# Program head of a four-layer trunk: vector loads moved to ScalarE's queue, vectors transposed between x's tiles, pool weight halves and y halves in turn

## The chip, the cores and the metric

The kernel runs on one core of one Trainium2 chip. The metric is the device time of one execution in microseconds, as the median of several runs. The engines are named as in the profile: PE is TensorE (PEld its weight loads), DVE is VectorE, ACT is ScalarE, POOL is GpSimd, SP is SyncE; SPq and ACTq are the instructions on SP and ACT that issue DMAs.

## The reference

A trunk of four layers on 16 meta tokens and 512 tokens of width 1024. Each layer is a mixer and a SwiGLU feed-forward, both with residual. The mixers are a pool mixer (layers 0 and 3), differential attention (layer 1) and a conformer convolution (layer 2). The program head ends in the first pool mixer:

```python
meta = jnp.broadcast_to(meta_tokens[None].astype(x.dtype), (B_, N_META, D_MODEL))
h = jnp.concatenate([meta, x], axis=1)
for i in range(DEPTH):
    mixer, j = i % N_MIXERS, i // N_MIXERS
    y = rmsnorm(h, norm_mix_g[i])
    if mixer == 0:
        y = pool_mixer(y, pool_w[j], pool_b[j], pool_scale[j])
    ...
    h = h + y
    h = h + swiglu_ffn(rmsnorm(h, norm_ffn_g[i]), ffn_w_gate[i], ffn_w_up[i], ffn_w_down[i])
return rmsnorm(h[:, N_META:], final_norm_g)

def pool_mixer(h, w, b, scale):
    # four groups of 256 channels: (trailing mean over 2, 4, 8, 16 tokens) - h, times a 256x256 matrix
    ...
    return (mixed + b) * scale
```

## The kernel before

Activations are kept transposed: `h` is [128 channels, 8 blocks x 528 tokens] in SBUF. Every product is made of three float32r products: each operand is split into a high part (`y_hi`, `w_hi`, made by ACT) and a rest (`y_lo`, `w_lo`, made by DVE), and PE multiplies high with high, high with low and low with high. Weights arrive in a ring `w_raw` of four slots; SP issues each load (`load`, L654) when the rest of the tile four before it has been made (`lo_ready`).

The program head does this. POOL clears `vec_rows` (L774) and `tok_x` (L775), builds the identity (L781) and then the band matrices of the trailing means (`bands_raw`, to L808). SP issues the rows of x in six loads (L634 to L638, token tiles 0 to 4, the last of 32 rows), then waits for `vec_zeroed` and issues twelve small loads of the norms' gains, biases and convolution taps into `vec_rows`, 50 rows of 1024 values (L644 to L649), then the four pool weights (through L654, 256 KB each), then four lambda vectors (L734) and the bias table (L736). PE runs six filler products (`unread`, L1709) and transposes x's five tiles (L1718), DVE copies each from PSUM to `h` (L3003). PE then runs six more fillers, transposes `vec_rows` into bank 7 (L1724), runs 15 fillers and waits for `vec_ready`, which DVE gives when it has copied the bank to `m.vec` (L3009). ACT meanwhile takes the sum of squares of each x tile (L2192, into `tok_x`) and splits the pool weights of groups 0 and 1 (L1795).

With `vec_ready` the pool layer begins. ACT makes `y_hi` of the eight channel blocks (L1800, a product with the norm's gain), with the splits of weights 2 and 3 behind blocks 1 and 3, and then rounds the band matrices (L1849). DVE makes the rests in the same order (L2342 for weights, L2348 for y), then the bands' rest (L2460), then the row factors, one reciprocal root for each token (`row_factors_of`, L2408 to L2411, from `token_sums`), and gives `tok_ready`. PE multiplies token tiles 0 to 2 group by group and then tiles 3 and 4 (L1034, `rows_times_weights`; the first product waits for `lo_ready` of group 0 and `y_ready` of blocks 0 and 1). When `tok_ready` is there, ACT scales each tile's result into `z_hi` (L1867), DVE makes `z_lo` (L2477). PE, after six fillers behind `z_ready` of two tiles (L1120), multiplies the z tiles with the bands (`windows`, L1073 to L1082; its first one waits for `z_ready` of four tiles), and between the blocks it begins layer 0's feed-forward (L972). DVE adds the windows to `h` (L2449). A DMA of the relative bias table goes out from ACT in that stretch (L1882, L2202), and from there on PE computes the feed-forward.

## Time and profile before

| | |
|---|---|
| median of 3 runs | 1990.15 us (1990.10 to 1990.54) |
| the profiled execution's own time | 1987.6 us |
| its span, first to last instruction | 1985.9 us |
| mean granted TensorE clock | 0.998 |
| PE busy | 1966.1 us, 99% of the span |
| DVE, ACT, POOL busy | 1573.7, 930.4, 207.7 us |

Times in the rows are microseconds from the span's start. A timeline row gives start, duration, engine, line, operation, out<-in, the count that was merged, and in brackets the idle time before it with what ended it. A row of the chain of waits gives start, duration and what the end of the program goes back to in that stretch. An idle engine costs time only where that chain passes over it.

### The profile page before, as it was taken

The page shows a single profiled execution, that of the slowest core. Times are in us where ns is not written, and L with a number is a line of the kernel's source. Part 1 is how long each engine was busy: PE and PEld are TensorE (multiplying, and loading weights), DVE is VectorE, ACT ScalarE, POOL GpSimd, SP SyncE. Part 2 cuts the span into 40 slices and gives each one's busy share as a digit, 9 for nine tenths or more (in the row PEclk, how much of TensorE's full clock was granted, in tenths as well). Part 3 has the DMA queues.
Part 4 walks back from the last instruction along what each step waited for, and adds up shares of the span by engine and source line. Part 5 has one row for each costly group of instructions (what it writes and reads, how often), then busy time and mean ns, then how long its engine had stood idle before and what let it go on. Part 6 is the DMA issues. An engine that isn't in the chain of part 4 may idle for free.

```text
span 1985.9 us, 39847 instructions
## 1 busy us (share of the span) xinstructions
PE 1966.1 (99%) x15706; PEld 1910.9 (96%) x15706; DVE 1573.7 (79%) x2188; ACT 930.4 (47%) x1475; POOL 207.7 (10%) x325
## 2 busy tenths in 40 slices
PE   9999999999999999999999989999999999999998
PEld 8999999999999999999999989999999998989997
DVE  6797788768788788877979987697778768977794
ACT  7443333346675534433447775343334454433342
POOL 5000000231111200000051212000000140000000
PEclk9999999999999999999999999999999999999999
DMA  5433243342111324233345762223343323423232
GB/s 171 140 86 106 84 127 85 92 124 65 53 57 56 91 86 128 79 90 105 91 115 126 163 131 64 86 86 106 84 127 85 113 70 106 116 76 106 86 105 96
DMA packets 305390, 196.82 MB, mean 99 GB/s; under 512 B 7450, under 2 KB 297243, under 8 KB 305012
## 3 DMA queue, kind: packets, MB, share of 16 engines
q1 hardware_dynamic: 298972, 175.08, 30.8%
q0 software_dynamic: 5104, 15.71, 3.8%
q10 hardware_dynamic: 1192, 4.34, 0.6%
q8 instruction: 84, 1.38, 0.3%
q14 instruction: 38, 0.31, 0.1%
HBM read 179.45 MB, written 6.44 MB: 94 GB/s over the span
## 4 chain that ended last, share of the span: by engine, by line
PE 87%; DVE 6%; ACT 3%; issue 3%; DVEq 1%; DMA 1%; SPq 0%; ACTq 0%
PE ps L972 43%; PE ps L1269 35%; PE ps L1380 2%; PE ps L1225 1%; DVE cv_odd L3098 1%; PE ps L1452 1%; DVE cv L3098 1%; PE ps L1082 1%; PE ps L1493 1%; PE ps L1034 1%; PE ps L1099 0%; PE ps L1481 0%; PE ps L1505 0%; DMA x_rows<-in_x 0%; DVE w_lo L2586 0%
## 5 line engine op out<-in xcount | busy, mean ns | idle before, releaser
L1269 PE MATMUL ps<-t_lo,y_hi 128*128 128x264 f32 (+1 forms) x1008 | 285.7, 283 | 0.0
L1269 PE MATMUL ps<-t_lo,w_hi 128*128 128x264 f32 (+1 forms) x1008 | 285.7, 283 | 0.0
L1269 PE MATMUL ps<-t_hi,w_lo 128*128 128x264 f32 (+1 forms) x1008 | 285.4, 283 | 0.0
L1269 PE MATMUL ps<-t_hi,y_lo 128*128 128x264 f32 (+1 forms) x1008 | 285.3, 283 | 0.0
L1269 PE MATMUL ps<-t_hi,w_hi 128*128 128x264 f32 (+1 forms) x1008 | 285.1, 283 | 0.1
L1269 PE MATMUL ps<-t_hi,y_hi 128*128 128x264 f32 (+1 forms) x1008 | 284.8, 283 | 0.0
L1927 ACT ACTIVATE w_hi<-w_raw 128x1024 fp32r<-128x1024 f32 (+1 forms) x108 | 127.8, 1201 | 329.6 <-PE ps L972 193.3
L972 PE MATMUL ps<-hid_hi,w_hi 128*128 128x264 f32 (+1 forms) x1184 | 265.3, 296 | 1.2 <-DVE hid_lo L2642 1.2
L972 PE MATMUL ps<-hid_lo,w_hi 128*128 128x264 f32 (+1 forms) x1184 | 264.6, 296 | 0.0
L972 PE MATMUL ps<-hid_hi,w_lo 128*128 128x264 f32 (+1 forms) x1184 | 264.2, 296 | 0.0
L972 PE MATMUL ps<-y_hi,w_hi 128*128 128x264 f32 (+1 forms) x1088 | 240.5, 297 | 0.6 <-issue 0.3
L972 PE MATMUL ps<-y_hi,w_lo 128*128 128x264 f32 (+1 forms) x1088 | 233.5, 291 | 0.0
L972 PE MATMUL ps<-y_lo,w_hi 128*128 128x264 f32 (+1 forms) x1088 | 233.5, 291 | 0.0
L1927 ACT ACTIVATE y_hi<-w_raw 128x1024 fp32r<-128x1024 f32 (+1 forms) x108 | 125.8, 1196 | 167.1 <-DVE w_raw L2596 133.9
L972 PEld LDWEIGHTS ps<-hid_hi,w_hi 128*128 128x128 f32 x1184 | 187.2, 188 | 7.3 <-DVE hid_lo L2642 1.6
L972 PEld LDWEIGHTS ps<-hid_lo,w_hi 128*128 128x128 f32 x1184 | 187.7, 188 | 5.5
L972 PEld LDWEIGHTS ps<-hid_hi,w_lo 128*128 128x128 f32 x1184 | 187.4, 188 | 5.7
L1269 PEld LDWEIGHTS ps<-t_hi,w_hi 128*128 128x128 f32 x1008 | 189.8, 188 | 0.6 <-DVE h L2682 0.5
L1269 PEld LDWEIGHTS ps<-t_hi,y_hi 128*128 128x128 f32 x1008 | 189.8, 188 | 0.0
L1269 PEld LDWEIGHTS ps<-t_lo,w_hi 128*128 128x128 f32 x1008 | 189.5, 188 | 0.1
L1269 PEld LDWEIGHTS ps<-t_hi,w_lo 128*128 128x128 f32 x1008 | 189.5, 188 | 0.0
L1269 PEld LDWEIGHTS ps<-t_hi,y_lo 128*128 128x128 f32 x1008 | 189.5, 188 | 0.0
(395 smaller groups left out, 4340.5 us busy)
## 6 DMA issues: line engine op xcount, KB each, us to landing
w_raw<-in_ffn_w_gate SPq DMA_DIRECT2D x88, 512.0 KB, 5.1
w_raw<-in_ffn_w_up SPq DMA_DIRECT2D x88, 512.0 KB, 4.7
w_raw<-in_ffn_w_down SPq DMA_DIRECT2D x70, 512.0 KB, 4.4
w_raw<-in_ffn_w_down SPq DMA_DIRECT2D x24, 384.0 KB, 4.4
w_raw<-in_attn_w_qkv SPq DMA_DIRECT2D x16, 512.0 KB, 3.8
w_raw<-in_conv_w_in SPq DMA_DIRECT2D x16, 512.0 KB, 4.1
w_lo<-w_raw POOLq DMA_DIRECT2D x16, 512.0 KB, 5.4
w_raw<-in_attn_w_qkv SPq DMA_DIRECT2D x16, 256.0 KB, 2.9
```

The costliest lines, as they stand in the source:

```text
L972: mm = pe.matmul(ps[:, bank + hf, 0:half], w[:, slot, col:col + P], x(hf), start=begin and w is m.w_hi and n == 0, stop=end and w is m.w_lo)
L1034: mm = pe.matmul(out, y[:, at:at + rows], w[:, (t0 + g) % SLOTS, k * 256:(k + 1) * 256], start=k == 0 and n == 0, stop=k == 1 and n == 2)
L1082: mm = pe.matmul(out[:, c0:c1], z, m.bands[0:TILE_ROWS[i], g, at:at + c1 - c0], start=i == 2 and n == 0, stop=i in (1, 4) and n == 1)
L1225: mm = pe.matmul(ps[:, 2 * g + hf, 0:HALF], w[:, (tile0 + g) % SLOTS, k * P:(k + 1) * P], x[:, at:at + HALF], start=k == 0 and n == 0, sto ...
L1269: mm = pe.matmul(ps[:, bank, 0:hw], w[:, at:at + P], b[:, t, k, 0:hw], start=k == 0 and n == 0, stop=k == 3 and n == 2)
L1380: mm = pe.matmul(bank, x, w, start=False, stop=k == LAST_F - 1 and n == 2)
L1452: mm = pe.matmul(ps[:, (4, proj_banks(par, 1))[part] + c, col:col + k1 - k0], q[rows, 0, q0:q0 + P], k[rows, 1, k0:k1], start=n == 0, stop ...
L1493: mm = pe.matmul(ps[:, 4, i * P:QT * P], v, w, start=False, stop=i == QT - 1 and x == 2)
L1927: act.activation(hi[:, sub * SUB:(sub + n_sub) * SUB], src, ACT.Copy).then_inc(s.op_hi, 1)
L3098: dve.scalar_tensor_tensor(out=sums[n % 2], in0=u, scalar=vec_col(ROW_DW + tap, c), in1=sums[n % 2], op0=ALU.mult, op1=ALU.add).then_inc(s ...
```

## The change

SP no longer issues the twelve vector loads: ACT does, before its first square, after the same wait for `vec_zeroed`. The pool weights' loads are thereby right behind x on SP. PE transposes the vectors after x's tile 2, with a semaphore of their own (`vec_turned`), before tile 3; the fillers before that transpose are gone and those behind tile 4 become 18 in place of 15. DVE copies the vectors behind tile 2's copies. ACT takes the squares of tiles 0 to 3 first; it splits each pool weight ahead of the two y blocks of its group, waits for `vec_ready` behind the first split, and takes the squares of tile 4 behind the eight y blocks. DVE's rests follow the same order.

```diff
@@ sync
-            sp.wait_ge(s.vec_zeroed, 1)
-            for row, name in ((ROW_MIX, "norm_mix_g"), ...):
-                sp.dma_start(m.vec_rows[row:row + n, :], a[name]).then_inc(s.vec_in, 16)
...
@@ tensor
                 mm.then_inc(s.rows_turned, 1)
-            unread(6)
-            pe.wait_ge(s.vec_in, 16 * 12)
-            for d in range(NB):
-                mm = pe.transpose(ps[:, 7, d * ROWS:(d + 1) * ROWS], m.vec_rows[:, d * P:(d + 1) * P],
-                                  m.ident[0:ROWS, 0:ROWS])
-            mm.then_inc(s.rows_turned, 1)
-
-            unread(15)
+                if i == 2:
+                    pe.wait_ge(s.vec_in, 16 * 12)
+                    for d in range(NB):
+                        mm = pe.transpose(ps[:, 7, d * ROWS:(d + 1) * ROWS], m.vec_rows[:, d * P:(d + 1) * P],
+                                          m.ident[0:ROWS, 0:ROWS])
+                    mm.then_inc(s.vec_turned, 1)
+
+            unread(18)
             pe.wait_ge(s.vec_ready, 1)
@@ scalar, pool_layer
-                    act.wait_ge(s.vec_ready, 1)
                     for d in range(NB):
+                        if d % 2 == 0:
+                            split_hi(tile0 + d // 2, 0, 0, cols[tile0 + d // 2])
+                        if d == 0:
+                            act.wait_ge(s.vec_ready, 1)
                         y_hi(d, H_IN, Y_POOL0, ROW_MIX + 0, 0, TOK)
-                        if d in (1, 3):
-                            split_hi(tile0 + (3 + d) // 2, 0, 0, cols[tile0 + (3 + d) // 2])
+                    row_squares(TILES - 1).then_inc(s.token_sums, 1)
                     act.wait_ge(s.band_built, 1)
@@ scalar, head
+            act.wait_ge(s.vec_zeroed, 1)
+            for row, name in ((ROW_MIX, "norm_mix_g"), ...):
+                act.dma_start(m.vec_rows[row:row + n, :], a[name]).then_inc(s.vec_in, 16)
...
             act.wait_ge(s.tok_cleared, 1)
-            for i, n in enumerate(TILE_ROWS):
+            def row_squares(i):
+                n = TILE_ROWS[i]
                 act.wait_ge(x_in[i], 32 if i == 0 else 16)
-                e = act.activation(m.row_squares[0:n, i, :], m.x_rows[0:n, i, :], ACT.Square,
-                                   accum_out=m.tok_x[0:n, i:i + 1])
-            e.then_inc(s.token_sums, 1)
-            for t in range(2):
-                split_hi(t, 0, 0, cols[t])
+                return act.activation(m.row_squares[0:n, i, :], m.x_rows[0:n, i, :], ACT.Square,
+                                      accum_out=m.tok_x[0:n, i:i + 1])
+            for i in range(TILES - 1):
+                row_squares(i)
@@ vector, pool_layer
-                    for c in (0, 1):
-                        split_lo(tile0 + c, 0, 0, cols[tile0 + c])
                     for d in range(NB):
+                        if d % 2 == 0:
+                            split_lo(tile0 + d // 2, 0, 0, cols[tile0 + d // 2])
                         y_lo(d, Y_POOL0, ROW_MIX + 0, 0, TOK)
-                        if d in (1, 3):
-                            split_lo(tile0 + (3 + d) // 2, 0, 0, cols[tile0 + (3 + d) // 2])
@@ vector, head
+                if i == 2:
+                    dve.wait_ge(s.vec_turned, 1)
+                    dve.tensor_copy(m.vec[:, :], ps[:, 7, 0:NB * ROWS]).then_inc(s.vec_ready, 1)
             e.then_inc(s.h_ready, NB)
-            dve.wait_ge(s.rows_turned, TILES + 1)
-            dve.tensor_copy(m.vec[:, :], ps[:, 7, 0:NB * ROWS]).then_inc(s.vec_ready, 1)
-            dve.drain()
+            dve.wait_ge(s.vec_ready, 1)
```

## Rows read from the trace of the kernel before

**Rows 1.** Chain of waits in order of time, to 120 us

```profile
2.67 7.40 DMA x_rows<-in_x
...
11.82 1.53 PE ps L1709 x12
...
14.02 0.58 DVE vec L3009
14.63 1.36 ACT y_hi L1800 x2
15.99 0.52 ACT w_hi L1795
...
20.79 2.73 ACT bands L1849
...
25.94 2.12 ACT z_hi L1867 x2
...
31.35 1.29 DVE z_lo L2477
...
32.69 0.39 PE ps L1073
...
59.22 58.65 PE ps L972 x480
```

**Rows 2.** Timeline of PE

```profile
10.12 1.70 PE L1718 MATMUL ps<-ident,x_rows 127*128 127x127 f32 x16 [1.10 <-DMA x_rows<-in_x]
...
13.91 3.62 PE L1709 MATMUL ps<-ones 128*128 128x128 f32 x30
17.58 0.35 PE L1034 MATMUL ps<-w_hi,y_hi 128*128 128x256 f32 x1
...
31.74 0.89 PE L1120 MATMUL ps<-z_hi 128*128 128x264 f32 x6
```

**Rows 3.** Timeline of ACT, its DMA issues (ACTq) among it

```profile
11.16 1.04 ACT L2192 ACTIVATE row_squares<-x_rows 32x1024 f32<-32x1024 f32 x1
...
13.24 1.36 ACT L1795 ACTIVATE w_hi<-w_raw 128x512 fp32r<-128x512 f32 x2 [0.95 <-DMA w_raw<-in_pool_w]
...
23.86 0.35 ACTq L1859 DMA_DIRECT2D bands_scratch<-bands  x1
...
31.94 1.11 ACT L1867 ACTIVATE z_hi<-ps,tok_r 32x1024 fp32r<-32x1024 f32 x1 [0.62 <-PE ps L1034]
...
54.36 0.53 ACTq L1882 DMA_DIRECT2D rel_once<-rel  x1
```

**Rows 4.** Timeline of DVE

```profile
7.31 3.56 DVE L3003 COPY h<-ps 128x512 f32<-128x512 f32 x6 [7.31 <-PE ps L1718]
11.24 1.68 DVE L3003 COPY h<-ps 128x508 f32<-128x508 f32 x4 [0.38 <-PE ps L1718]
...
27.09 2.48 DVE L2477 SCALAR_TENSOR_TENSOR z_lo<-ps,tok_r,z_hi 128x1024 fp32r<-128x1024 f32 x2 [0.40 <-ACT z_hi L1867]
```

**Rows 5.** Timeline of POOL and of SP's queue: `vec_rows` cleared, first vector load, pool weights' loads

```profile
0.81 0.94 POOL L774 MEMSET vec_rows<- 50x1024 f32 x1 [0.29 <-POOLq L3212]
...
3.63 0.38 SPq L644 DMA_DIRECT2D vec_rows<-in_norm_mix_g  x1
...
7.52 1.93 SPq L654 DMA_DIRECT2D w_raw<-in_pool_w  x4
```

**Rows 6.** Stretches: start:end, length, busy (PE, PEld, DVE, ACT, POOL), PEclk, DMA share, GB/s

```profile
3.00:8.50 5.50, 5.50 (x33) 5.50 (x34) 1.19 (x2) 3.11 (x4) 5.14 (x36) 1.00 1.02 381
8.50:10.25 1.75, 0.65 (x6) 0.41 (x5) 1.75 (x5) 1.55 (x5) 1.62 (x5) 1.00 1.06 152
1162.20:1166.30 4.10, 0.10 (x2) 0.00 (x0) 2.40 (x5) 3.24 (x9) 0.00 (x0) 1.00 1.09 261
1166.30:1172.00 5.70, 5.63 (x66) 5.66 (x68) 5.67 (x10) 5.65 (x7) 0.83 (x2) 0.70 0.05 9
```

**Rows 7.** Page, DMA issues: KB each, median us from issue to landing

```profile
lam_rows<-in_attn_lambda_k SPq DMA_DIRECT2D x2, 32.0 KB, 6.3
```

More of the change, by code:

```diff
@@ L367, in __init__ @@
         self.rows_turned = sem("rows_turned")
+        self.vec_turned = sem("vec_turned")
         self.turned_read = sem("turned_read")
@@ L638, in _ @@
                 sp.dma_start(m.x_rows[0:n, i, :], a["x"][0, t:t + n, :]).then_inc(x_in[i], 16)
-            sp.wait_ge(s.vec_zeroed, 1)
-            for row, name in ((ROW_MIX, "norm_mix_g"), (ROW_FFN, "norm_ffn_g"), (ROW_POOL_B, "pool_b"),
-                              (ROW_POOL_S, "pool_scale"), (ROW_DWB, "conv_dw_b"), (ROW_LNG, "conv_ln_g"),
-                              (ROW_LNB, "conv_ln_b"), (ROW_CONV_OUT, "conv_b_out")):
-                n = a[name].shape[0]
-                sp.dma_start(m.vec_rows[row:row + n, :], a[name]).then_inc(s.vec_in, 16)
-            sp.dma_start(m.vec_rows[ROW_CONV_IN:ROW_CONV_IN + 2, :],
-                         a["conv_b_in"].rearrange("o (r n) -> (o r) n", r=2)).then_inc(s.vec_in, 16)
-            for t, n in ((0, 16), (16, TAPS - 16)):
-                sp.dma_start(m.vec_rows[ROW_DW + t:ROW_DW + t + n, :], a["conv_dw_w"][0, t:t + n, :]).then_inc(s.vec_in, 16)
-            sp.dma_start(m.vec_rows[ROW_SUBLN:ROW_SUBLN + 1, 0:P], a["attn_subln_g"]).then_inc(s.vec_in, 16)
             def load(off, i, per, src, at_col, width):
@@ L2186, in attention_step @@
                         split_hi(first["attn_out"] + NB + c, 0, 0, 512)
+            act.wait_ge(s.vec_zeroed, 1)
+            for row, name in ((ROW_MIX, "norm_mix_g"), (ROW_FFN, "norm_ffn_g"), (ROW_POOL_B, "pool_b"),
+                              (ROW_POOL_S, "pool_scale"), (ROW_DWB, "conv_dw_b"), (ROW_LNG, "conv_ln_g"),
+                              (ROW_LNB, "conv_ln_b"), (ROW_CONV_OUT, "conv_b_out")):
+                n = a[name].shape[0]
+                act.dma_start(m.vec_rows[row:row + n, :], a[name]).then_inc(s.vec_in, 16)
+            act.dma_start(m.vec_rows[ROW_CONV_IN:ROW_CONV_IN + 2, :],
+                         a["conv_b_in"].rearrange("o (r n) -> (o r) n", r=2)).then_inc(s.vec_in, 16)
+            for t, n in ((0, 16), (16, TAPS - 16)):
+                act.dma_start(m.vec_rows[ROW_DW + t:ROW_DW + t + n, :], a["conv_dw_w"][0, t:t + n, :]).then_inc(s.vec_in, 16)
+            act.dma_start(m.vec_rows[ROW_SUBLN:ROW_SUBLN + 1, 0:P], a["attn_subln_g"]).then_inc(s.vec_in, 16)
             act.wait_ge(s.tok_cleared, 1)
-            for i, n in enumerate(TILE_ROWS):
+            def row_squares(i):
+                n = TILE_ROWS[i]
                 act.wait_ge(x_in[i], 32 if i == 0 else 16)
-                e = act.activation(m.row_squares[0:n, i, :], m.x_rows[0:n, i, :], ACT.Square,
-                                   accum_out=m.tok_x[0:n, i:i + 1])
-            e.then_inc(s.token_sums, 1)
-            for t in range(2):
-                split_hi(t, 0, 0, cols[t])
+                return act.activation(m.row_squares[0:n, i, :], m.x_rows[0:n, i, :], ACT.Square,
+                                      accum_out=m.tok_x[0:n, i:i + 1])
+            for i in range(TILES - 1):
+                row_squares(i)
             pool_layer("pool0", 0, R_POOL0, Y_POOL0, H_POOL0, Y_FFN0, ROW_FFN + 0)
```

## The prediction

> **What bounds the kernel now.** The page has PE busy for 99% of the span, so only a stretch in which the end does not depend on PE's own work can give time back. I read the chain of waits of the first 120 us to find such stretches, then the timelines of PE, ACT and DVE over the same time to see how close the next engine is, and last SP's queue with the stretches of DMA traffic.
>
> The chain [rows 1] begins with the load of x's tile 3, landed at 10.07 (2.67 + 7.40). It goes through the transposes of tiles 3 and 4 [rows 2], six fillers that take 1.53 before the vectors are transposed, and DVE's copy of the vectors (0.58) to `vec_ready`. At 14.63 it enters ACT and stays: y blocks and two weight splits to 20.79, the bands for 2.73, a short row-factor chain on DVE, `z_hi` from 25.94, the fourth `z_lo` (ends 32.64), and only then PE's windows at 32.69. From there PE runs with next to no gap into the long stretch at 59.22 [rows 1]. PE's first pool product, at 17.58 [rows 2], is not in the chain at all. PE ends that stage at 31.74, and its six fillers, some 0.7 us, bring it to about 32.5, so it has only a few tenths to spare against the 32.69 of the chain.
>
> The quantity to forecast is therefore when the fourth `z_lo` is ready. It comes 32.64 - 14.63 = 18.01 after the first `y_hi`.
>
> **What the change does to ACT between the first y_hi and z_hi.** Before, weights 0 and 1 were split while ACT waited for the vectors (it began at 13.24), and the square of tile 4 was done at 11.16 [rows 3]. Now the split of weight 1 stands behind the first two y blocks and the square behind the last. A split in a row of ACT's work takes 0.52 (the one at 15.99, [rows 1]), and the square 1.04 [rows 3]. The bands, and the row factors that need the tile's sum as well, wait behind them. The fourth `z_lo` then comes 18.01 + 0.52 + 1.04 = 19.57 after the first `y_hi`. To be as early as now, 32.64, the first `y_hi` must begin at 13.07: 1.56 earlier than now. All the saving at the top of the program has to pay this first.
>
> DVE does as many rests as before; in its new order each pair follows ACT's pair and the bands' rest follows ACT's bands, so it adds nothing to this chain.
>
> **When the first y_hi can begin.** It needs three things; the last one decides.
>
> (a) All of `h`. DVE's copies of tiles 3 and 4 end 11.24 + 1.68 = 12.92 [rows 4], which is 2.85 after tile 3 of x lands at 10.07. The next instruction on ACT starts some 0.06 later, so this says 12.98 plus whatever tile 3 is late.
>
> (b) DVE's own order. Tiles 0 to 2 end at 7.31 + 3.56 = 10.87 [rows 4]. The vectors' copy of 0.58 [rows 1] now comes next, and the last copies take 1.68: 13.13, or 13.19 with the same 0.06. The copy used to run alone behind them; in the old gap of 0.38 [rows 4] it fits only in part.
>
> (c) Weight 0. ACT waited until 13.24 for it [rows 3]; with 0.52 for its split this gives 13.76. Its load is now issued at 3.63 in place of 7.52 [rows 5], but x and the same vectors are still moved ahead of it or beside it by engines that were full. Between 11.5 and 13.24 is my bracket; the lower end takes off the 1.75 us of the slow stretch [rows 6].
>
> So even if nothing is late, (b) gives 13.19, 0.12 after the break-even.
>
> **How late x's tile 3 comes.** The vectors' loads stood behind x in SP's queue. ACT now issues them from 0.81 + 0.94 = 1.75 on, when `vec_rows` is cleared, while x is being moved. SP needed 3.63 to 7.52 for the twelve, 0.32 each [rows 5]. ACT's issues take 0.35 and 0.53 where the trace has them, for larger transfers [rows 3]; with 0.32 to 0.53 each ACT is done between 5.6 and 8.1. Its squares follow, and it waits for tile 3 of x before the last of them in any case, unless the issues are at the long end. The vectors' packets are thus all in the machine before tile 3 is complete. While x is moved the transfers run at 381 GB/s with all engines' time taken; in the stretch behind x they run at 152 GB/s, again with all of it taken, for 1.75 us [rows 6]. The vectors are 50 rows of 4 KB, 0.2 MB. At x's rate they cost x 0.54 us; if their rows are as slow beside x as behind it they cost the whole 1.75. No row tells between them, nor excludes 0 if they slip into gaps. I take 1.1, the middle of 0.54 and 1.75, since some of the engines that served few of the short loads should go on with x.
>
> Here a rule of the Trainium skill speaks against the change: DMA: Bandwidth & Descriptors, section "Issuing engines are not separate DMA queues", says that transfers issued by different engines run on the same 16 DMA engines and interleave, which saves only the issuing time. By that rule tile 3 is late; if a second issuer were a second lane, it would land at 10.07 still and the sum would go by (b) or (c).
>
> With 1.1, (a) gives 14.08, above (b) and above (c) at its latest. 14.08 - 13.07 = +1.0 us at the fourth `z_lo` and so at PE's windows, 33.7 in place of 32.69.
>
> **PE.** Its old 6 + 15 fillers become 18. Tiles 3 and 4 are transposed 1.7 after tile 3 lands, so by 12.9; a pass takes 3.62/30 = 0.12 [rows 2], 36 passes 4.4, and the first product comes at about 17.3, 0.3 earlier than now. At the stage's length of 14.16 (17.58 to 31.74) it ends near 31.4; its second `z_lo` is ready at 29.57 [rows 4] plus 1.0, the six fillers end at 32.2, and PE then stands for 1.5 us. ACT's wait of 0.62 for PE before the last `z_hi` [rows 3] goes; that shortens the last tile's part, which PE needs only 2 us later. The vectors' transposes (8, under 0.7) lie in the old gap of 1.10 before tile 3 [rows 2], which is longer now; if it is gone, they cost 0.7. Behind 32.69 PE is dense to 59.22, so the delay stays to the end.
>
> SP's pool, lambda and table loads are issued 3.9 earlier (7.52 to 3.63) and, beyond weight 0, nobody on the chain waits for them; the feed-forward's first tiles are freed by `lo_ready` as before and are wanted only near 38. These I cost at nothing.
>
> **Sum.** -1.56 needed, first `y_hi` 0.55 earlier (14.63 to 14.08): +1.0 us on the profiled execution's 1987.6, that is 1988.6 there. The median of the runs was 1990.15, 2.55 above that execution, so 1991.2.
>
> **Rivals.**
> 1. *x isn't held up.* Tile 3 lands by 10.3 and (b) or (c) decides: +0.1 to +0.7, 1990.3 to 1990.8. For it: the issues spread over several us and the rate of 152 may be latency that overlaps. Against: the engines' time was all taken.
> 2. *The vectors are late.* PE's transposes of tile 3 now stand behind `vec_in`. Small loads in a full queue took 6.3 to land [rows 7]; issued last at 5.3 that is 11.6, then 14.02 - 11.82 - 1.53 = 0.67 for their transposes [rows 1], and 2.85 to the end of the copies: first `y_hi` at 15.2, +2.1, 1992.2. With issues at 0.53 it is near +3 to +5. It decides from a landing at about 10.6 on.
> 3. *PE's start decides after all* (faster). If the z chain had slack that the chain view hides, the stage would move with PE's first product: tile 3 at 10.07 + 1.7 + 4.4 = 16.2, 1.4 earlier, 1988.8. It needs the fourth `z_lo` by 31.2, so the first `y_hi` by 11.7; (a) to (c) all speak against it.
> 4. *The clock.* PE's wait of about 1.5 us before the windows grows with the delay. After the one long wait in this trace, 4.1 us, the granted clock was 0.70 over 5.70 us [rows 6], a share of it at the 1.2 GHz level: 1.7 us lost. The gap of 1.10 at 9 us was followed by no fall. With +1.0 this gives +2.7, 1992.9. The Trainium skill (TensorE: Matmul & The Clock Gate, "Part 1: The HAM clock gate") has the clock halved after an idle time, and by it this rival is possible wherever PE is made to stand.
>
> **Chances and range.** Forecast (x held up by 0.5 to 1.75, +0.5 to +1.7) 0.50; rival 1 0.20; rival 2 0.13; rival 3 0.07; rival 4 0.10. A range from 1988.7 to 1993.2 leaves out part of rivals 2 and 3 and what no case covers. A change of 0.2% is 4 us here, about what can be told from no change, and every listed case but the long end of rival 2 or rivals 2 and 4 together stays within it: slower 0.06, faster 0.04, same 0.90.
>
> **What the profile of after would show.** x's tile 3 landing near 11.2 and the first `y_hi` near 14.1; ACT's bands ending near 24.5; `z_hi` from 26.9; the first pool product near 17.3 and a gap of some 1.5 us on PE before the windows at 33.7, with clock 1.00. A landing at 10.1 with the first `y_hi` at 13.2 to 13.8 is rival 1; a gap on PE between the tile 2 and the vectors' transposes that outlasts tile 3's landing is rival 2; windows before 32.5 would make the prediction wrong in sign.

## The result and the profile after

The change makes the kernel slower: a median of 1994.91 us against 1989.39 us for the kernel before on the same chip (15 runs each), ratio 1.0028 with a 95% interval of 1.0021 to 1.0035, so some 5.5 us. The prediction was 1991.2 within 1988.7 to 1993.2, that is +1.0 on the kernel before. The profiled execution took 1994.83 us, its span is 1993.1 us and its mean granted clock 0.996 (before 0.998).

The chain of waits of the kernel after, to 120 us (start, duration, what):

```profile
5.74 7.57 DMA vec_rows<-in_attn_subln_g
13.36 1.09 PE ps L1713 x8
14.45 2.87 PE ps L1707 x16
17.32 7.07 PE ps L1698 x36
24.39 14.08 PE ps L1023 x120
38.47 0.73 PE ps L1109 x6
...
65.57 54.54 PE ps L961 x445
```

L1713 is the transpose of the vectors, L1707 that of x, L1698 the fillers, L1023 the pool products, L1109 the fillers ahead of the windows, L961 the feed-forward. Where the chain of before began with the load of x's tile 3 and crossed ACT and DVE from 14.63 to 32.69 [rows 1], it now begins with the last of the vectors' loads and stays on PE all the way to the windows and through them (to 59.8). The windows begin at 39.20, behind the six fillers, and the long stretch at 65.57 in place of 59.22: 6.35 us later. That is more than the 5.5 us between the medians and most of the 7.2 between the two profiled executions, so the loss lies in the program head.

The timeline of PE (in brackets the idle time before and what ended it):

```profile
8.69 1.09 PE L1707 MATMUL ps<-ident,x_rows 128*128 128x128 f32 x8 [0.93 <-DMA x_rows<-in_x]
13.36 1.09 PE L1713 MATMUL ps<-ident,vec_rows 50*128 50x50 f32 x8 [3.57 <-DMA vec_rows<-in_attn_subln_g]
14.38 2.94 PE L1707 MATMUL ps<-ident,x_rows 127*128 127x127 f32 x16
17.25 7.14 PE L1698 MATMUL ps<-ones 128*128 128x128 f32 x36
```

PE stands for 3.57 us in front of the vectors. Behind that, the transposes of tiles 3 and 4 take 2.94 where they took 1.70, and 36 filler passes take 7.14 where 30 took 3.62 [rows 2]. The stretches say why (start:end, length, busy PE, PEld, DVE, ACT, POOL, then PEclk, DMA share, GB/s):

```profile
10.25:13.30 3.05, 0.00 (x0) 0.00 (x0) 0.74 (x2) 1.53 (x4) 2.90 (x8) 0.96 1.08 280
14.40:17.30 2.90, 2.90 (x18) 2.51 (x17) 1.50 (x3) 0.00 (x0) 0.46 (x2) 0.50 0.12 22
17.30:24.20 6.90, 6.90 (x38) 6.90 (x37) 6.73 (x14) 6.06 (x11) 6.90 (x17) 0.57 0.52 146
24.20:38.30 14.10, 14.10 (x122) 13.95 (x121) 9.69 (x23) 9.77 (x10) 4.17 (x16) 1.00 0.56 196
```

The granted clock is 0.50, the 1.2 GHz level, for the transposes and most of the fillers, and 1.00 again from the first product on. ACT and DVE in the same time:

```profile
5.74 0.27 ACTq L2190 DMA_DIRECT2D vec_rows<-in_attn_subln_g  x1
...
11.90 1.06 ACT L2197 ACTIVATE row_squares<-x_rows 127x1024 f32<-127x1024 f32 x1 [1.27 <-DMA x_rows<-in_x]
13.55 0.63 ACT L1784 ACTIVATE w_hi<-w_raw 128x512 fp32r<-128x512 f32 x1 [0.50 <-DMA w_raw<-in_pool_w]
18.14 1.36 ACT L1789 ACTIVATE y_hi<-h,vec 128x528 fp32r<-128x528 f32 x2 [3.96 <-DVE h L3006]
...
25.77 2.81 ACT L1840 ACTIVATE bands<-bands_raw 128x3132 fp32r<-128x3132 f32 x1
...
31.57 2.12 ACT L1858 ACTIVATE z_hi<-ps,tok_r 128x1024 fp32r<-128x1024 f32 x2 [2.99 <-PE ps L1023]
```

```profile
16.37 1.68 DVE L3006 COPY h<-ps 128x508 f32<-128x508 f32 x4 [1.31 <-PE ps L1707]
...
29.02 0.60 DVE L2360 TENSOR_SCALAR tok_r<-tok_x 128x5 int32<-128x5 int32 x1
...
36.98 1.28 DVE L2480 SCALAR_TENSOR_TENSOR z_lo<-ps,tok_r,z_hi 127x1024 fp32r<-127x1024 f32 x1 [0.35 <-ACT z_hi L1858]
```

ACT's square of tile 3 begins at 11.90, so that tile of x landed at 11.87 (9.2 us after its issue, before 7.40 [rows 1]). Weight 0 is there at 13.5, no earlier than before (13.24 [rows 3]), though it was issued 3.9 us sooner; it decides nothing. The first `y_hi` begins at 18.14 (before 14.63). The fourth `z_lo` ends at 38.26, so the z chain alone would have let the windows begin at 38.3; PE, which ends its products at 38.47 and its fillers at 39.20, adds 0.9.

### The profile page after: what moved, and what is told of

Its sections match the earlier page's. It is cut to its first block, busy times and chain, and to the rows that moved or that the text cites. A ratio compares the mean times of both kernels' runs of the same rounds, so it can differ in the third digit from the quotient of the medians.

```text
span 1993.1 us, 39834 instructions
## 1 busy us (share of the span) xinstructions
PE 1969.3 (99%) x15700; PEld 1914.1 (96%) x15700; DVE 1574.3 (79%) x2188; ACT 930.3 (47%) x1475; POOL 211.2 (11%) x325
## 3 DMA queue, kind: packets, MB, share of 16 engines
q10 hardware_dynamic: 1292, 4.55, 0.6%
## 4 chain that ended last, share of the span: by engine, by line
PE 86%; DVE 6%; issue 3%; ACT 2%; DVEq 1%; DMA 1%; POOL 0%; ACTq 0%; POOLq 0%; SPq 0%
PE ps L961 41%; PE ps L1258 35%; PE ps L1369 2%; PE ps L1023 1%; PE ps L1214 1%; DVE cv_odd L3102 1%; PE ps L1441 1%; DVE cv L3102 1%; PE ps L1071 1%; PE ps L1482 1%; PE ps L1088 0%; PE ps L1494 0%; PE ps L1470 0%; DMA vec_rows<-in_attn_subln_g 0%; PE ps L1698 0%
## 5 line engine op out<-in xcount | busy, mean ns | idle before, releaser
L961 PE MATMUL ps<-hid_hi,w_hi 128*128 128x264 f32 (+1 forms) x1184 | 265.4, 296 | 1.7 <-DVE hid_lo L2645 1.7
L961 PE MATMUL ps<-hid_lo,w_hi 128*128 128x264 f32 (+1 forms) x1184 | 264.7, 296 | 0.0
L961 PE MATMUL ps<-hid_hi,w_lo 128*128 128x264 f32 (+1 forms) x1184 | 264.1, 296 | 0.0
L961 PE MATMUL ps<-y_hi,w_hi 128*128 128x264 f32 (+1 forms) x1088 | 240.6, 297 | 0.5 <-issue 0.3
L961 PE MATMUL ps<-y_lo,w_hi 128*128 128x264 f32 (+1 forms) x1088 | 233.6, 291 | 0.0
L961 PE MATMUL ps<-y_hi,w_lo 128*128 128x264 f32 (+1 forms) x1088 | 233.5, 291 | 0.0
L961 PEld LDWEIGHTS ps<-hid_hi,w_hi 128*128 128x128 f32 x1184 | 187.2, 188 | 8.3 <-DVE hid_lo L2645 2.4
L961 PEld LDWEIGHTS ps<-hid_hi,w_lo 128*128 128x128 f32 x1184 | 187.5, 188 | 5.6
L961 PEld LDWEIGHTS ps<-hid_lo,w_hi 128*128 128x128 f32 x1184 | 187.6, 188 | 5.5
```

What stands on the lines that cost most here:

```text
L961: mm = pe.matmul(ps[:, bank + hf, 0:half], w[:, slot, col:col + P], x(hf), start=begin and w is m.w_hi and n == 0, stop=end and w is m.w_lo)
```

## The experiments

Windows, landings and first instructions below are read from each run's own timeline and chain; "late" and "early" are against the kernel before (windows at 32.69, long stretch at 59.22). A time "+9.2" is from issue to landing. The medians of the kernel before were 1988.7 to 1990.1 us in the batches. Where SP issues the vectors, tile 3 of x lands at +6.3 (e10) to +7.4 (before) although nothing in its loads differs, so a shift of half a microsecond between two profiles can be chance.

**First group: which part of the change costs.** Four kernels.

e1: after, with 16 more fillers in front of the wait for the vectors.

```diff
                 if i == 2:
+                    unread(16)
                     pe.wait_ge(s.vec_in, 16 * 12)
```

> The changed kernel, and in it 16 more fillers on PE between the transposes of x's tile 2 and the wait for the vectors, where PE stood idle for 3.57 us. Theory (wait and clock): the vectors land at 13.3 and hold the transposes of tiles 3 and 4, and after PE has stood there the granted clock is halved (0.50 from 14.4 to 17.3, 0.57 to 24.2), so that two tiles' transposes take 2.94 and the 18 fillers 7.14 us. With the clock kept at 1.00 the transposes take 1.7 and the fillers 4.3, the first pool product comes at 20.0 to 20.5 in place of 24.15, and the z chain on ACT then decides: windows near 36.5 in place of 39.0. That is 2 to 3 us faster than the changed kernel and 3 to 4 slower than before. Rival (traffic and order alone, the clock only goes with them): windows stay near 39.0 because something else holds them, and the time stays 5.5 us above before.

Ratio 1.0023 (1.0013 to 1.0032). The timeline of PE:

```profile
10.13 3.74 PE L1698 MATMUL ps<-ones 128*128 128x128 f32 x32
13.80 0.70 PE L1714 MATMUL ps<-ident,vec_rows 50*128 50x50 f32 x8
14.43 1.70 PE L1707 MATMUL ps<-ident,x_rows 127*128 127x127 f32 x16
16.06 4.29 PE L1698 MATMUL ps<-ones 128*128 128x128 f32 x36
```

With PE kept at work the clock stays at 1.00: the transposes take 1.70 again, the 36 passes 4.29, the first product comes at 20.10 and not at 24.15. The windows begin at 37.38, only 1.8 earlier than after's, because the z chain behind a `y_hi` at 17.32 takes over. So the clock is a part of the loss, 1.8 of the 6.5 us at the windows, and not the larger one.

e2: after, with the vectors' transposes (and DVE's copy) behind tile 4 in place of tile 2.

```diff
-                if i == 2:
+                if i == TILES - 1:
                     pe.wait_ge(s.vec_in, 16 * 12)
```

> The changed kernel with the vectors transposed behind tile 4 in place of behind tile 2, and copied by DVE behind tile 4's copies; the loads stay on ACT. Theory (the place of the wait holds tiles 3 and 4): tile 3 lands at 11.9, both tiles are transposed by 13.6, the vectors by 14.2, first y_hi near 15.3 in place of 18.14, fourth z_lo near 34.9; with PE idle only from 9.8 to 11.9 the clock stays up and the first pool product comes near 18.7. Windows near 35, 2 to 3 us slower than before, 3 to 4 faster than the changed kernel. Rival (the order of waits is nothing, the vectors' landing alone holds everything): first y_hi stays near 17 to 18 and the time within 1 us of the changed kernel's.

Ratio 1.0016 (1.0006 to 1.0025); windows at 35.25. Its timeline of PE:

```profile
12.28 1.70 PE L1707 MATMUL ps<-ident,x_rows 127*128 127x127 f32 x16 [2.64 <-DMA x_rows<-in_x]
13.90 0.70 PE L1713 MATMUL ps<-ident,vec_rows 50*128 50x50 f32 x8
14.53 5.91 PE L1698 MATMUL ps<-ones 128*128 128x128 f32 x36
```

Tiles 3 and 4 are transposed and copied while the vectors are on their way, the first `y_hi` begins at 15.59, and 3.95 of the 6.5 us at the windows are back. This is the largest share: the place of the wait. It is not clear of the clock's, since the transposes run at full speed here too (1.70 for 2.94), so the 3.95 here and the 1.8 of e1 overlap. What stays is tile 3 at 12.23 (+9.6), the wait of 2.64 for it, the lower clock behind it (5.91 for 36 passes), and the order on ACT: 15.59 - 14.63 = 0.96 at the first `y_hi` and 1.6 for the order (e8) make up the 2.56 by which the windows are still late.

e3: before, with nothing changed but that ACT issues the twelve loads.

```diff
-            sp.wait_ge(s.vec_zeroed, 1)      # and the twelve loads
+            act.wait_ge(s.vec_zeroed, 1)     # and the twelve loads, ahead of tok_cleared
```

> The kernel before with one edit: ACT issues the twelve vector loads, so that the pool weights are right behind x on SP; all orders on PE, ACT and DVE as before. Theory: x's tile 3 lands at 11.9 as in the changed kernel (1.8 later), the vectors at 13.3, first y_hi near 16.4, windows near 34.5: 1.5 to 2.2 us slower than before. Rival (the loads' move is worth something and the new waits spoil it): tile 3 at 11.9, but the first y_hi not later than 14.9 and the time within 0.5 us of before.

Ratio 1.0021 (1.0011 to 1.003); windows at 38.02, far from the 34.5 expected. Tile 3 lands at 12.0 (+9.3), and the timeline of PE shows what followed:

```profile
12.05 2.95 PE L1707 MATMUL ps<-ident,x_rows 127*128 127x127 f32 x16 [2.23 <-DMA x_rows<-in_x]
14.93 2.93 PE L1698 MATMUL ps<-ones 128*128 128x128 f32 x12
17.79 1.09 PE L1713 MATMUL ps<-ident,vec_rows 50*128 50x50 f32 x8
```

A wait of 2.23 was enough for the granted clock to fall to 0.50 (12 to 18.5 us), and transposes and fillers that lie on this kernel's path ran at half speed. The move of the loads alone gives a loss nearly as large as the whole change, 5.3 of 6.5 us at the windows.

e4: after, with the twelve loads back on SP behind x.

```diff
-            act.wait_ge(s.vec_zeroed, 1)     # and the twelve loads
+            sp.wait_ge(s.vec_zeroed, 1)      # and the twelve loads, behind x's
```

> The changed kernel with the twelve vector loads back on SP behind x and ahead of the pool weights; the new orders on PE, ACT and DVE stay. Theory (place of the wait, and clock): tile 3 lands at 10.1 again, the vectors at 11.5 to 13, PE stands before them for 2.5 to 4 us and the clock may fall as it did; with the clock down windows at 37 to 39, with it up 35 to 36. The time is 3 to 6 us above before although ACT issues nothing. Rival (traffic: ACT's loads beside x are the cause): windows within 1 us of before's 32.7.

Ratio 1.0025 (1.0015 to 1.0035). x's tile 3 lands at 9.6 again (+6.9), but the vectors land at 13.56 (issued 7.25, +6.31), PE waits 4.69 for them, the clock is 0.50 behind it, the first `y_hi` comes at 18.39 and the windows at 38.43. Against after's 13.31 the vectors are 0.25 later for an issue 1.5 later: the earlier issue bought next to nothing, and neither queue is right with the wait at this place. The parts do not add up: the loads alone cost 5.3 (e3), the orders and the wait's place without them 5.7 (e4), all together 6.5. In each of the three PE has one wait of over 2 us and a clock of 0.50 behind it.

**Second group: the landings, and the order of ACT.**

e5: after, with SP holding the pool weights until the vectors are in.

```diff
+            sp.wait_ge(s.vec_in, 16 * 12)
             load_pool("pool0", 0)
```

> The changed kernel, with SP waiting for the vectors before it issues the pool weights; read for landings, not for time. In the runs so far the vectors landed at 13.3 to 13.6 whoever issued them (last issue 5.74 on ACT, 7.25 on SP). Theory A (the pool weights' packets, issued from 3.6 on, share the engines with the vectors): without them the vectors land before 11.9, where tile 3 of x did. Theory B (the vectors' own rows are slow, the rest of the traffic doesn't matter much): they still land at 12.5 to 13.3. In both the first pool weight lands some 3 to 4 us after its issue, so the first y_hi comes near 17 to 18 and the time is as bad as the changed kernel's.

One execution, 1997.05 us. Stretches:

```profile
8.50:10.00 1.50, 1.09 (x8) 0.86 (x8) 1.26 (x3) 1.50 (x4) 1.37 (x5) 1.00 0.97 208
10.00:11.50 1.50, 0.00 (x0) 0.00 (x0) 0.93 (x2) 0.60 (x2) 1.50 (x7) 1.00 0.30 66
11.50:13.00 1.50, 0.00 (x0) 0.00 (x0) 0.00 (x0) 1.15 (x2) 1.35 (x3) 0.85 0.02 9
```

The traffic falls to 9 GB/s, the DMA engines are all but idle from 11.5 on, and yet the vectors' last load counts as landed only at 13.09 (after: 13.31), tile 3 at +9.1. The pool weights beside them are thus not what makes either late. The share is a mean over 16 engines: 0.30 does not exclude that one or two of them still had a queue.

e6: after, with the vector loads of one and two rows issued row by row, each row cut into 16 pieces, so that more DMA engines serve them (15 loads in all).

```diff
-                act.dma_start(m.vec_rows[row:row + n, :], a[name])
+                act.dma_start(m.vec_rows[row:row + 1, :].rearrange("p (a b) -> p a b", a=16),
+                              src.rearrange("o (a b) -> o a b", a=16))
```

> The changed kernel, with each of the ten vector loads of one row or two rows (biases, scales, gains) issued as rows of 16 pieces of 256 B, one load for each row, 15 loads in all; the two of four rows and the taps' two as before. Theory B (single rows of 4 KB pile up at one place in the machine, about 11 of them one behind the other): in pieces they spread, tile 3 of x lands near 10.5 and the vectors before 11.5; PE's wait before them shrinks from 3.57 to under 1.7, the clock stays at 1.00, and with the first y_hi near 14.5 the windows come at 34 to 35 in place of 39.0: 3 to 4 us faster than the changed kernel. Theory A (it is the amount of traffic): landings stay within 0.5 us of 11.9 and 13.3, and so does the time.

Ratio 1.0032 (1.0019 to 1.0044). ACT's loads add 100 packets to their queue (1292 against 1192), as before the edit, so by this count the rows were moved in the same pieces and the premise was not tested; three more loads made the last issue 6.75 and the landing 14.04.

e7: e3 with ten fillers between tiles 2 and 3.

```diff
+                if i == 2:
+                    unread(10)
```

> The kernel before with ACT issuing the vector loads (as in the run of that edit alone, whose windows came at 38.0) and 10 fillers on PE between the transposes of tiles 2 and 3. Theory (of the 5.3 us that the loads' move alone cost, the 1.9 of tile 3's lateness are traffic and the rest is the clock, which fell after PE's wait of 2.23): the transposes of tiles 3 and 4 take 1.7 again, first y_hi at 16.3 to 16.6, windows at 34.4 to 34.8, about 3.4 us faster than without the fillers and 1.8 slower than before. Rival (the clock falls whatever PE does there, or something else is late): windows stay at 37 to 38.

Ratio 1.0018 (1.0008 to 1.0027). The clock is 1.00, the transposes take 1.70, `y_hi` begins at 17.32 (e3: 19.53) and the windows at 35.54 (e3: 38.02). So at least 2.2 of the 4.9 us by which e3's first `y_hi` was late are the clock. Of the 2.48 at the windows another 0.43 is one operation on DVE (`tok_r`, see below). Tile 3 was later here than in any other run, 12.75 (+10.1), 0.74 behind e3's, which is why 34.8 was missed.

e8: before, with the change's order on ACT and DVE and nothing else.

```diff
                     for d in range(NB):
+                        if d % 2 == 0:
+                            split_hi(tile0 + d // 2, 0, 0, cols[tile0 + d // 2])
                         y_hi(d, H_IN, Y_POOL0, ROW_MIX + 0, 0, TOK)
-                        if d in (1, 3):
-                            split_hi(tile0 + (3 + d) // 2, 0, 0, cols[tile0 + (3 + d) // 2])
+                    row_squares(TILES - 1).then_inc(s.token_sums, 1)
```

> The kernel before with the new order on ACT and DVE alone: weight and y halves in turn, the square of tile 4 behind the eight y blocks. Loads, transposes and fillers as before. Theory (the term of 0.52 + 1.04 of the prediction): first y_hi stays at 14.6, the row factors and z_hi come 1.56 later (27.5 in place of 25.94), windows at 34.2 in place of 32.7: 1.5 us slower. Rival (the alternation lets PE begin earlier and the rest follows): first pool product at 17.0, windows at or before 32.7, the time within 0.5 us of before.

Ratio 1.0014 (1.0004 to 1.0023); windows at 34.46 and long stretch at 61.01, both 1.8 late. The timeline of ACT:

```profile
14.81 1.36 ACT L1800 ACTIVATE y_hi<-h,vec 128x528 fp32r<-128x528 f32 x2 [0.52 <-DVE vec L3011]
...
21.41 1.05 ACT L2196 ACTIVATE row_squares<-x_rows 32x1024 f32<-32x1024 f32 x1
22.45 2.82 ACT L1851 ACTIVATE bands<-bands_raw 128x3132 fp32r<-128x3132 f32 x1
...
27.71 2.12 ACT L1869 ACTIVATE z_hi<-ps,tok_r 128x1024 fp32r<-128x1024 f32 x2 [2.44 <-DVEq L2415]
```

`z_hi` stands 12.90 behind the first `y_hi`, where it stood 11.31 (25.94 - 14.63, [rows 1]). The prediction's term for this order was +1.56; measured +1.59.

The first `y_hi` is 0.18 late as well. PE's row for the vectors' transposes shows why, although its loads and fillers are those of the kernel before:

```profile
13.47 0.70 PE L1724 MATMUL ps<-ident,vec_rows 50*128 50x50 f32 x8 [0.77 <-DMA vec_rows<-in_attn_subln_g]
```

Tile 3 was early here (+6.7), the six fillers were done sooner, and the wait for the vectors stood behind them; they landed at 13.43.

**Third group: the loads themselves.**

e9: after, with `vec_rows` laid out with a gap behind each 128 values, so that a row can't be one run of 4 KB (the loads of two rows are issued row by row, 15 in all). e10: the same rows in the kernel before, without its six fillers ahead of the vectors.

```diff
-        self.vec_rows = new("vec_rows", [ROWS, D])
+        self.vec_rows = new("vec_rows", [ROWS, NB, P + 8])
```

> The changed kernel with vec_rows laid out as 8 pieces of 128 values with 8 unused ones behind each, so that a row's load can't be one run of 4 KB at its destination; loads of two rows are issued row by row, 15 loads in all. The run with the pieces laid end to end changed nothing in the packets (100 on ACT's queue, as before). With the pool weights held back, the vectors' traffic fell to 23 GB/s from 11 us on, a seventeenth of the full rate, and the vectors landed at 13.1 all the same. Theory B (single rows of 4 KB queue at one of the engines, about 11 behind each other): the packets on ACT's queue rise well above 100, the tail goes, the vectors land by 11.8 and PE's wait before them is under 2 us. Theory C (the landing at 13.1 to 13.6 is a fixed cost of twelve or more loads in flight, not of where their bytes go): it stays at 13 or later.

> The kernel before (loads on SP behind x, old order on ACT and DVE, vectors transposed behind tile 4) with the same laid-out rows, 15 loads, and without the six fillers ahead of the vectors' transposes. Theory B: the vectors land by 12, the first y_hi begins at 13.3 to 14.0 in place of 14.63, the fourth z_lo and the windows come about 0.6 to 1.3 earlier, at 31.7 to 32.2: up to 1 us faster than before, hardly measurable in the time. Theory C: the vectors land at 13 or later, the first y_hi stays at 14.5 to 15.

e9: ratio 1.0041 (1.0027 to 1.0055); e10: 1.0007 (0.9998 to 1.0017). Most issues now cost their queue 0.62 to 0.68 us in place of some 0.3, so e9's last is issued at 12.11 and lands at 17.27, e10's at 13.59 and 15.35. The slower issuing outweighs what smaller pieces may give, so these two say nothing on how the rows are spread. They do show that a load issued last into a quiet machine lands in 1.76. In e10 PE stood 4.21 us for the vectors, the clock fell to 0.50 and the profiled execution (1992.74 us) has its long stretch at 63.88, 4.7 late, while the median is only 1.7 above that of the kernel before; a profile is one execution, and the record doesn't explain this gap.

e11: before, with the six fillers ahead of the vectors' wait moved behind it.

```diff
-            unread(6)
             pe.wait_ge(s.vec_in, 16 * 12)
...
-            unread(15)
+            unread(21)
```

> The kernel before with its six fillers ahead of the vectors' transposes moved behind them (0 and 21 in place of 6 and 15). The prediction took the 1.53 us of these fillers as time on the chain. Theory now: they only covered the wait for the vectors, which land at 13.3 to 13.6 anyway; the transposes stay at 13.3 or later, PE's wait of some 1.5 us appears in the trace, the first y_hi stays at 14.6 and, with PE idle only for that, the clock stays at 1.00 or nearly; the first pool product comes 0.7 later. Rival (as the prediction had it): transposes at 11.8 to 12.2 and the first y_hi near 13.8.

One execution, 1989.52 us, first `y_hi` at 14.33 (0.30 early) and windows at 33.23 (0.54 late). The timeline of PE:

```profile
5.50 5.72 PE L1718 MATMUL ps<-ident,x_rows 128*128 128x128 f32 x40
12.86 0.70 PE L1723 MATMUL ps<-ident,vec_rows 50*128 50x50 f32 x8 [1.63 <-DMA vec_rows<-in_attn_subln_g]
13.49 4.96 PE L1709 MATMUL ps<-ones 128*128 128x128 f32 x42
```

This bares what the fillers hid in the kernel before: the vectors land at 12.81 with SP's loads too (7.28 + 5.53). The fillers' 1.53 us on the chain [rows 1] were a cover for this wait, and at most 0.5 of them was real. What the first `y_hi` gained was lost again on PE: with 21 fillers behind the vectors its products ended at 32.5, and PE decided the windows.

e12: after, without the loads of the convolution's biases and layer-norm vectors (five of twelve; the convolution layer computes with zeros in their place).

> The changed kernel without the loads of conv_dw_b, conv_ln_g, conv_ln_b, conv_b_out and conv_b_in (their rows stay zero, so the convolution layer computes something else): seven loads are left. Theory B (rows of 4 KB one behind the other at one engine, 0.27 us each by the packets' share): 5 rows fewer there, the vectors land 1.3 to 2 us earlier, near 11.5, and tile 3 of x near 11. Theory C': the number of issues matters; the last issue is at 4.3 in place of 5.74 and the landing moves by the same 1.4, which alone can't be told from B; but tile 3 of x, issued at 2.7, moves only under B.

One execution, 1992.3 us; the first `y_hi` is at 15.42. The last issue is at 4.24 and lands at 11.84, +7.60: as long after its issue as with twelve. Tile 3 lands at 12.2, +9.5: not earlier. PE waits 2.29 and the clock falls behind it (36 passes in 7.15).

**Fourth group: what holds tile 3, and whether the aim can be had.**

e13: before, with two vector loads (8 rows) on ACT, ten on SP. e14: before, with the two tap loads (31 rows) on ACT. e15: after, with ACT issuing the vectors behind its square of x's tile 2.

> Kernel before, with two of the twelve vector loads (the two gains of four rows) issued by ScalarE while x is moved, the other ten by SyncE behind x. It asks how much of the lateness of x's tile 3 (6.3 to 7.4 us after its issue with SyncE's loads, 8.8 to 10.1 with ScalarE's) a small dose brings. Theory A, the delay is the work of the small rows (12 loads cost about 2 us): 8 rows of 50 cost 0.3 us, tile 3 lands 7.0 to 7.5 after its issue. Theory B, the delay comes with any second issuer beside x, whatever it loads (a run with seven loads showed it whole): tile 3 lands 8.8 or more after its issue, PE idles 2 us or more behind tile 2, the clock falls, and the windows begin near 36 or later.

> Kernel before, with the two tap loads (31 of the 50 rows, as two loads) issued by ScalarE while x is moved. Theory A by rows: 31 of 50 rows cost 1.2 us, tile 3 lands 8 to 8.5 us after its issue. Theory A by loads: 2 of 12 loads cost 0.3, so 7.0 to 7.5. Theory B (any second issuer): 8.8 or more.

> Kernel after, with ScalarE issuing the vector loads behind its square of x's tile 2 instead of at the start, so at about 8.5 to 9 us, when most of x is in. If what holds x's tile 3 is the vectors' packets beside x, tile 3 lands at +7.4 or earlier again (about 10). The vectors then land about 6 to 7.5 behind the last issue (near 13), that is at 19 or later, and PE waits for them ahead of tile 3: first y_hi at 23 or later, windows near 43, time about 10 us above the kernel before. If tile 3 lands at +9 all the same, the vectors beside x are not what holds it, and the pool weights issued close behind x are.

One execution each: 1989.79, 1991.17 and 2001.59 us; windows at 33.87, 33.89 and 43.84. From the chains of waits of e13 and of e14:

```profile
2.67 8.36 DMA x_rows<-in_x
```

```profile
2.68 8.38 DMA x_rows<-in_x
```

Two loads put tile 3 at +8.4, whether they bring 8 rows or 31; seven (e12) at +9.5, twelve or more at +8.8 to +10.1 (7.9 in e9, which issues more slowly); in e15, with no vector load beside x, no load of x took more than 7.7, although the pool weights stood right behind it. So the delay comes from the vector loads beside x. It goes neither with the rows (8 and 31 give the same) nor is it there in full with any second issuer: both theories fall in their pure form. e15's vectors land at 18.80, 5.22 after the last issue, and PE stood 9.36.

e16: before, with the vectors in two parts. SP issues the four loads that the pool layer reads (12 rows), then the pool weights, then the other eight; PE transposes 12 rows right behind tile 4 and all 50 behind group 0 of the products; DVE copies the rest of them behind its last y rest.

```diff
@@ sync: four loads, load_pool("pool0", 0), eight loads on vec_in2
@@ tensor
-            unread(6)
-            pe.wait_ge(s.vec_in, 16 * 12)
+            pe.wait_ge(s.vec_in, 16 * 4)
             for d in range(NB):
-                mm = pe.transpose(ps[:, 7, d * ROWS:(d + 1) * ROWS], m.vec_rows[:, d * P:(d + 1) * P], ...)
+                mm = pe.transpose(ps[:, 7, d * ROWS:d * ROWS + 12], m.vec_rows[0:12, d * P:(d + 1) * P], ...)
```

> Candidate to beat both: kernel before, with SyncE issuing behind x only the four vector loads that the pool layer reads (12 rows), then the pool weights, then the other eight with a semaphore of their own. PE transposes the 12 rows directly behind tile 4 (no six fillers) and all 50 rows behind group 0 of the pool products; DVE copies the rest of the vectors behind the last y rest. Theory: the four loads land about 6 us behind their issue, near 11, so the transposes of tile 4 end the wait; the first y_hi begins at 13.3 to 13.6 in place of 14.63, if weight 0 lands by 12.4 (issued 2.6 earlier); the windows begin near 31.6 in place of 32.69, and the time is 1.0 us below the kernel before, ratio 0.9995, at the edge of what can be told. Rival: weight 0 lands at 13.2 as before since x and the vectors are served first: the first y_hi at 14.3, no gain. Second rival: the eight late loads land after about 19, PE waits for them between the pool groups, the windows come at 33 or later, and the time is that of the kernel before or up to 2 us above.

Ratio 1.0 (0.999 to 1.0009). The first `y_hi` came 1.5 us earlier, at 13.11, and weight 0 was in by 12.07, but the windows stayed at 32.71. From the timelines of PE, DVE and POOL:

```profile
16.84 0.36 PE L1039 MATMUL ps<-w_hi,y_hi 128*128 128x256 f32 x1 [1.26 <-DVE y_lo L2359]
```

```profile
12.91 1.22 DVE L3029 TENSOR_TENSOR pool_bs<-vec 128x16 f32<-128x16 f32 x1
14.06 1.28 DVE L2353 TENSOR_TENSOR w_lo<-w_raw,w_hi 128x512 fp32r<-128x512 f32 x2
```

```profile
11.77 2.33 POOL L813 TENSOR_TENSOR bands_raw<-bands_raw,ident 128x512 f32<-128x512 f32 x2 [0.15 <-issue]
```

The z chain is 0.87 earlier (fourth `z_lo` ends at 31.77), and PE's products, held by DVE until 16.84, end at 31.98 and the fillers at 32.71. The bound has gone over to PE, which neither of the two rivals stated for e16 had named.

e17: e16, with the change's own order on DVE (rest of a weight, then the two y rests of its group) and one filler in place of six ahead of the windows.

```diff
-                    for c in (0, 1):
-                        split_lo(tile0 + c, 0, 0, cols[tile0 + c])
                     for d in range(NB):
+                        if d % 2 == 0:
+                            split_lo(tile0 + d // 2, 0, 0, cols[tile0 + d // 2])
                         y_lo(d, Y_POOL0, ROW_MIX + 0, 0, TOK)
...
-                        unread_rows(6)
+                        unread_rows(1)
```

> The kernel e16 with two more edits: DVE makes the rest of weight 1 behind the first two y rests (the change's own order on DVE) instead of ahead of them, and PE runs one filler in place of six before the windows. In e16 the z chain came 0.87 us earlier (fourth z_lo ended at 31.77, before 32.64), but PE's first product at 16.84 waited for DVE, its products ended at 31.98 and the six fillers of 0.73 brought the windows to 32.71: PE had become the bound. Theory: the first product no longer waits for the second weight's rest, some 0.6, and begins at about 16.2; the products end at 31.4, one filler later is 31.5, and the fourth z_lo at 31.8 decides: the windows begin at 31.8, 0.9 us earlier than in the kernel before, ratio 0.9995, at the edge of what can be told. Rival: POOL's additions until 14.1, beside which DVE's small product took 1.22 in place of 0.18, hold DVE and the later groups wait for y rests, so that the products end no earlier than 31.98: windows at 32.1, 0.6 earlier.

Ratio 0.9989 (0.998 to 0.9998): 1986.81 against 1989.13 us, faster than the kernel before by an interval that only just leaves out 1, and so than both. From the chain of waits:

```profile
30.16 1.29 DVE z_lo L2490
31.50 0.38 PE ps L1085
...
58.28 58.82 PE ps L977 x480
```

The first product starts at 16.04, the windows at 31.50 and the long stretch at 58.28, 1.19 and 0.94 early. The trace accounts for about 1 of the 2.3 us of the medians; the interval (0.4 to 4 us) holds both. Part of it may be chance: tile 3 landed at +6.6 here, +7.1 in e16 and +7.4 in the kernel before, and the first `y_hi` is 0.34 ahead of e16's. The rival was half right on DVE: beside POOL's additions, which ended at 14.64, the first two y rests took 2.36 in place of 1.43, but the products did end early enough.

## Why the prediction was wrong

**The step that failed** is the sentence in the part on PE, "The vectors' transposes (8, under 0.7) lie in the old gap of 1.10 before tile 3 [rows 2], which is longer now". It costs the transposes and takes the vectors as there. They landed at 13.31, 7.57 after the last issue, 1.4 after tile 3; PE stood 3.57 in front of them with tile 3 in SBUF, and everything behind it moved. e2 shows its size: with the wait (and DVE's copy) behind tile 4 and nothing else changed, 3.95 us of 6.5 come back at the windows, the clock's share in it included.

**Behind it stands a misreading of before.** I took the six fillers' 1.53 us on the chain as the cost that the change removes. A filler in the chain in front of a wait that shows no idle time can hide that the wait was just met. e11 took them away and the vectors' landing stood there, at 12.81; e8 has it at 13.43 with the fillers still in place. The kernel before had arranged tiles 3 and 4 (1.70) and the fillers over this wait; the change took both covers away and moved the wait to where nothing covers it.

**Rival 2 had the mechanism and too small a price.** It put the landing at 11.6 from 6.3 for a small load [rows 7], and gave +2.1, or +3 to +5. The landing was 7.57 after an issue at 5.74; +3.5 at the first `y_hi`. With the measured landing its own sum gives 13.31 + 0.67 + 2.85 + 0.06 = 16.89, +3.8 at the fourth `z_lo`, about 1994.0; the first `y_hi` came 1.25 later still, and 0.82 of that is the clock (e1). It left out rival 4, which did happen, at another place: I expected a wait of 1.5 us before the windows to lower the clock, and none was there (PE was dense from 13.36 on); it fell behind the wait for the vectors. e1 shows its share: 1.8 us at the windows. I named the two together only as a case outside the range and gave them no chance of their own, though here the one wait brought on both.

**The x tile** (1.1 taken, 0.54 to 1.75 as bounds): 11.87 - 10.07 = 1.8, just above the upper bound, and against the +6.9 of e4 it is 2.3. By the rule of the Trainium skill that the prediction weighed (DMA: Bandwidth & Descriptors, "Issuing engines are not separate DMA queues") the tile is late, and the trace agrees with 1.8. But my reasoning by rows and rate was wrong, since seven loads cost as much as twelve and 8 rows as much as 31. The upper bound was also misread from [rows 6]: the stretch from 8.50 to 10.25 is not behind x, whose tile 3 landed at 10.07 in it, and 0.2 MB at 152 GB/s are 1.35 us and not 1.75.

**Right:** the order on ACT (+1.56 forecast, +1.59 in e8), and with it the length of the z chain, 19.57 forecast and 19.59 in e2. Weight 0 came at 13.5, outside my bracket of 11.5 to 13.24, and decided nothing.

**The z chain of after** is 20.12. Of the 0.55 above the forecast 0.13 is ACT's wait for PE's products before `z_hi`, and 0.43 is one operation on DVE, `tok_r`, at 0.60 for 0.17. At the same time POOL clears a tile:

```profile
29.05 0.54 POOL L809 MEMSET sumsq<- 128x528 f32 x1 [1.22 <-DVE tok_x L2413]
```

The prediction had no term for this. POOL had finished its copies of the bias table, waited for DVE's step before `tok_r` and started together with it. In all seven traces with a `tok_r` of 0.60 (after, e1, e3, e4, e6, e9, e15) POOL's clearing begins 0.03 or 0.04 behind its start and ends with it; in the other twelve, with 0.17 or 0.18, it begins when `tok_r` is over. No run changed this by itself.

**Still open:** why the last of the small loads counts as landed 7.3 to 7.6 us after its issue from ACT (e5, after, e12), with the traffic all but gone for the last 1.5 us in e5, where SP's took 5.5 to 6.3; and why two loads cost tile 3 a microsecond and seven two. By e5 it is not the bandwidth taken by the pool weights; the spreading of rows over DMA engines stayed untested, since by the packets e6 did not change it, and e9 and e10 changed the cost of issuing.

## What to carry to other kernels

Before a wait is moved forward, find when its data lands, not when its waiting instruction ran: a filler or other work that ends just at the wait hides the landing, and one run with the cover taken away shows it. A small transfer issued earlier need not be in earlier (0.25 us for 1.5 here, between e4 and after), and it can delay the large one beside it; splitting off what is needed first (e16, e17) moved the first `y_hi` forward (1.5 and 1.9 us) where moving the issuer moved it back. Look also at what another engine will do once the order shifts: here POOL's clearing fell onto a step of the critical chain. When a chain is shortened by a microsecond, look at what has half a microsecond of slack and shorten that too, or the gain stays invisible, as between e16 and e17.

## What the runs showed of the hardware

- **Clock.** Waits of PE of 2.23 (e3), 2.29 (e12), 2.64 (e2), 3.42 (e5), 3.57 (after), 4.21 (e10), 4.30 (e6) and 4.69 us (e4) were each followed by a granted clock of 0.50 to 0.61, the 1.2 GHz level for most of the time, back at 1.00 by 24.2 in after; behind waits of 1.10 (before), 1.39 (e13), 1.48 (e7) and 1.63 us (e11) it stayed at 1.00. The fall can come late: in e2 and e12 the first operations behind the wait ran at full speed (0.70 for the vectors' transposes) and the fillers after them did not. That PE was full of work did not help at once: 36 passes took 7.14 in after and 7.15 in e12, 4.29 at full clock.
- **DVE beside POOL.** A product on 128x16 took 1.22 us in e16 and 0.58 in e17 while POOL's addition into the bands ran, against 0.18 in after behind it, and in e16 it ended as that addition did (14.1). The copies of tiles 3 and 4 from PSUM, which overlap it in part, kept their 1.68. In e17 POOL's own additions took 2.87 in place of 2.33. The `tok_r` of 0.60 beside POOL's clearing, in seven traces of seven and in none of the other twelve, is of the same kind. That the one engine held the other is argued from these rows; no run was made for it.
- **Issuing.** A load whose rows are laid out in eight separate pieces costs the issuing queue 0.62 to 0.68 us but for the first (e9, e10), a plain one 0.25 to 0.33 but for the first (before, after). Cutting a row into 16 contiguous pieces left the packets at 100 (e6, after).
